# Turning the MLP operand row by row behind the out-projection, preparing the first head earlier, and scalar forms of small products

## Chip, cores and metric

One core of a Trainium2 chip. The metric is the device time of one launch in microseconds (us); a program's time is the median of its runs.

## What is computed

One step of a streaming encoder trunk with two layers, on 1024 prompt rows and 32 sample rows of width 1024, in float32. Cut to what matters here:

```python
def layer_norm(x):
    mu = jnp.mean(x, axis=-1, keepdims=True)
    var = jnp.mean(jnp.square(x - mu), axis=-1, keepdims=True)
    return (x - mu) * lax.rsqrt(var + LN_EPS)
# per layer:  mix  = three groups of attention heads A, B, C (6 + 5 + 5 heads of 64)
#             sub-layer: x <- LayerNorm(alpha * x + gate(c) * sublayer(LN0(x) * (1 + scale(c)) + shift(c)))
# sublayer 1: concat(group_rms(A), group_rms(B), group_rms(C)) @ w_out
# sublayer 2: squared-ReLU MLP, 1024 -> 4096 -> 1024
# group A: p = exp(s - m) / (sum(exp(s - m)) + exp(sink - m)), with a learned sink for each head
```

LN0 is a LayerNorm without gain, so each layer has two norms behind one another: that of the sub-layer's sum (with gain and bias), and that of the next sub-layer's input (with scale and shift). Newest keys and values of all rows are outputs as well.

## The kernel before

All products of matrices run in three passes on the tensor engine: each float32 operand is split into a rounded part and the rest (`hi` and `lo`), and hi x hi, lo x hi and hi x lo are summed in PSUM. The splitting is work of ACT, DVE and POOL (GpSimd). Rows are handled in 9 row tiles: 8 of 128 prompt rows (NPT = 8) and one of 32 sample rows (NTT = 9, index NPT). The activations are also kept turned (columns on the partitions) as `u_hi` and `u_lo`.

Each layer is a series of blocks, and a block ends only when all engines have ended theirs:

- Projections (SP's list at L1014 to L1050, `low_parts` and `products` on POOL, `project` on PE, `query` and the value copies of L1245 on DVE). Queries and keys come out turned, values by row tile. While values are projected, the keys are turned back (L1095), copied by DVE to `k_stage` (L1253, two halves per row tile, `k_st` in the code) and stored by SP (`store_k`); the copy for tile t waits until the stores of tile t-1 have read the stage. In the same time the sums of the conditioning matrices are made: SP loads `w_ada_v` (`sp_conditions`, L283), and each such load waits until DVE's products of an earlier one (L292) are done. SP is one list worked off in order: a wait in it holds all behind.
- Prompt attention. For each of 16 heads POOL splits queries and values (L1402 to L1418), SP loads a bias (`bias`), POOL masks its corners by two memsets, PE scores (L1440), DVE adds the bias and takes the row's maximum (L1564, `logits`), ACT takes exponentials, PE turns the probabilities and multiplies by the values. The first head's keys are split by ACT (L1492) and DVE (L1536) in this block; then DVE makes `minus_sink`, `ident_r` and `causal_r` (L1538 to L1541). PE's first score waits for the two last named. At the end of each head of group A, DVE adds `esk` to `den`, 128x8 at once (L1589).
- Sample attention.
- Out-projection block (L1936 on). The operand is turned column tile by column tile (`turned_feed`), interleaved with the first three row tiles' matmuls; then PE does row tiles 3 to 8 one after another (L1982), each as soon as DVE has read the PSUM of the row tile three before. Per row tile DVE multiplies by the gate, adds to the old rows and takes mean and variance (`sum_rows`: L744, L746, L387, L389, L755); ACT takes the root of the variance (`roots`: L689, L691); DVE refines it (`refine`: L761, L763, L765, L768 or L770); ACT applies the norm (`norm`, L702); POOL applies gain and bias (`chain_pool`: L676, L678); ACT sums the rows and their squares (`second_sums`, L709 to L713, and `second_roots`), DVE refines (`second`), and ACT applies the second norm. The sample's tile comes last and is done by DVE alone. SP loads the old rows, then the first MLP chunk (`w_raw`, 1 MB, chunk UP0), then stores the rows between the norms (L659). POOL splits chunk UP0 when its chain is done.
- MLP block (L2080 on). It starts by turning the operand: `turned_feed` again, PE transposing a column tile of all rows (L436), ACT reading it, DVE splitting it, and PE multiplying with chunk UP0 (L453). Chunk UP0+1 is loaded at the block's start and split by POOL when the operand is done. Then the MLP runs chunk by chunk (L378).
- Between the layers, and at the end, a block of the same chain on the MLP's result (`chain_dve`, `chain_act`, `chain_pool`). Between the layers POOL also splits weights (L357, L359) in between; at the end there is no second norm.

The orders on ACT and DVE in the chain:

```python
for k in range(NTT if final else NPT + 3):          # ACT
    if k < NTT: roots(k)
    if 2 <= k < NPT + 2 and not final:
        second_sums(k - 2); second_roots(k - 2)
    if k < NPT:
        act.wait_ge(f_fig, NTT * u + k + 1); norm(k, f_yn)
    if k >= 3 and not final:
        ...
        norm(k - 3, f_xn)
for k in range(NTT):                                # DVE
    sum_rows(k)
    if k >= 3 and not final: second(k - 3)
    ...
    refine(k, None, f_fig)
```

Of the kernel before, what the change touches and what calls it, by code (L numbers as in the profile page):

```python
# [17 lines left out]
F32 = mybir.dt.float32  # L18
# [48 lines left out]
def build(nc, io):  # L67
# [28 lines left out]
    with ExitStack() as ctx:  # L96
# [62 lines left out]
        u_lo = at("u_lo", U0 + 33792, [P, KT, T], F32R)  # L159
        qk = at("qk_t", Q0, [P, Q_TILES + K_TILES, T])  # L160
# [32 lines left out]
        ks_hi = [at(f"keys_hi{s}", D0 + 4096 * s, [P, SEQ], F32R) for s in range(2)]  # L193
        ks_lo = [at(f"keys_lo{s}", D0 + 8192 + 4096 * s, [P, SEQ], F32R) for s in range(2)]
# [3 lines left out]
        q_st = [at(f"queries{s}", W0 + 4096 * s, [P, SEQ], F32R) for s in range(2)]  # L198
        bias_h = [at(f"bias{s}", W0 + 8192 + 4096 * s, [P, SEQ]) for s in range(2)]
# [347 lines left out]
        f_st = [S(f"rows_stored{i}") for i in range(4)]  # L547
# [17 lines left out]
        GROUPS = ((0, 384), (384, 320), (704, 320))  # L565

# [85 lines left out]
        def chain_stores(sp, u, dst, first, last):  # L652

            for t in range(first, last):
                if t < NPT:
                    sp.wait_ge(f_x1, NPT * u + t + 1)
                else:
                    sp.wait_ge(f_last, u + 1)
                sp.dma_start(dst(t), x_all[0:rows_of(t), t, :]).then_inc(f_st[t % 4], 16)  # L659

        def stored(t, u):

            return 16 * ((3 if t % 4 == 0 else 2) * u + t // 4 + 1)

        def chain_stored(sp, uses):

            for i in range(4):
                sp.wait_ge(f_st[i], 16 * uses * (3 if i == 0 else 2))
# [62 lines left out]
        def chain_dve(own, u, rows, loaded, gate, after_sums, final):  # L731
# [25 lines left out]
            def refine(t, minus_mean, done):  # L757
# [7 lines left out]
                own.did(dve.tensor_tensor(scale, scale, r0, ALU.mult))  # L765
# [3 lines left out]
                else:  # L769
                    ins = dve.tensor_tensor(shift, minus_mean, scale, ALU.mult)  # L770
# [40 lines left out]
            dve.wait_ge(f_st[0], stored(NPT, u))  # L811
# [112 lines left out]
        for l in range(DEPTH):  # L924
# [60 lines left out]

            with nc.Block() as block:
                @block.sync
                def _(sp):
# [64 lines left out]
                def _(pool):  # L1053
# [24 lines left out]
                    for n in range(2, IN_CH):  # L1078
                        low_parts(n)
                        if n < 8:  # L1080
                            products(done, done + (4, 4, 3, 4, 4, 1)[n - 2])
                            done += (4, 4, 3, 4, 4, 1)[n - 2]

# [57 lines left out]
                def _(act):  # L1141
# [46 lines left out]
                    high_part(9)  # L1188

                @block.vector  # L1190
                def _(dve):
# [107 lines left out]
                    query(6)  # L1299
                    query(7)  # L1300
# [14 lines left out]
            span = {"a": 2, "b": 5, "c": NPT}  # L1315
# [12 lines left out]
            with nc.Block() as block:  # L1328
                @block.sync
                def _(sp):  # L1330
                    def bias(hn):
                        g, h = heads[hn][0:2]
                        if hn >= 2:
                            sp.wait_ge(d_lg, NPT * (hn - 1))
                        if g == "a":
                            dst, src = bias_h[hn % 2][:, 0:2 * P], bass.AP(scr_a.tensor, h * P * EXT_A + 127,
                                                                           [[EXT_A - 1, P], [1, 2 * P]])
                        elif g == "b":
                            dst, src = bias_h[hn % 2][:, 0:5 * P], bass.AP(scr_b.tensor, (l * BH + h) * (P * EXT_B) + 127,
                                                                           [[EXT_B - 1, P], [1, 5 * P]])  # L1340
                        else:
                            if h == 0:
                                sp.wait_ge(b_fout, 32)
                            dst, src = bias_h[hn % 2][:].rearrange("p (i t) -> p i t", t=P), \
                                bass.AP(scr_f.tensor, h * P, [[0, P], [CH * P, NPT], [1, P]])
                        sp.dma_start(dst, src).then_inc(d_bias[hn % 2], 16)

# [962 lines left out]
```

## Time and profile before

| what | us |
|---|---|
| median of 3 runs (lowest, highest) | 3181.93 (3179.59, 3183.39) |
| the profiled execution, its own time | 3183.84 |
| span of that execution in the trace | 3182.1 |
| TensorE (PE) busy | 2924.9, 92% of the span |
| DVE, POOL, ACT busy | 1581.2, 1525.1, 875.0 |

In layer 0 the projections end and prompt attention starts at 345.1 us, the out-projection block begins at 642 and the MLP block at 792.3, the block between the layers at 1553; layer 1 follows some 1565 us behind. The last block begins at 3119. The time of a run is about 1.7 us more than the span, which the trace doesn't show. In a timeline row the first number is the start, the second the duration; the brackets say how long the engine was idle before and what released it. A wait of the tensor engine that names "PEq L1936" ended with the end of the block before.

### The profile page before, as it was taken

The page shows a single profiled execution, that of the slowest core. Times are in us where ns is not written, and L with a number is a line of the kernel's source. Part 1 is how long each engine was busy: PE and PEld are TensorE (multiplying, and loading weights), DVE is VectorE, ACT ScalarE, POOL GpSimd, SP SyncE. Part 2 cuts the span into 40 slices and gives each one's busy share as a digit, 9 for nine tenths or more (in the row PEclk, how much of TensorE's full clock was granted, in tenths as well). Part 3 has the DMA queues.
Part 4 walks back from the last instruction along what each step waited for, and adds up shares of the span by engine and source line. Part 5 has one row for each costly group of instructions (what it writes and reads, how often), then busy time and mean ns, then how long its engine had stood idle before and what let it go on. Part 6 is the DMA issues. An engine that isn't in the chain of part 4 may idle for free. (4 is left out here: it accounts for less than half of the span.)

```text
span 3182.1 us, 46999 instructions
## 1 busy us (share of the span) xinstructions
PE 2924.9 (92%) x18646; PEld 2792.0 (88%) x18646; DVE 1581.2 (50%) x3177; ACT 875.0 (27%) x1710; POOL 1525.1 (48%) x716
## 2 busy tenths in 40 slices
PE   5999899887999999999979998998979999999993
PEld 5999789675999999999979897985859999999993
DVE  6552587556433333333775518775653333333347
ACT  1341476425210010011253307663341010001001
POOL 2693497235333443434339818953334443444334
PEclk5999899988999999999769999997989999999996
DMA  5441211431111111110534502114211111111112
GB/s 227 166 167 60 73 48 44 142 114 58 58 41 53 40 52 40 45 47 26 208 142 145 175 14 87 53 45 148 108 55 54 40 53 40 53 40 50 42 47 89
DMA packets 117352, 253.63 MB, mean 80 GB/s; under 512 B 42564, under 2 KB 78952, under 8 KB 103700
## 3 DMA queue, kind: packets, MB, share of 16 engines
q1 hardware_dynamic: 110868, 228.58, 21.0%
q10 hardware_dynamic: 6336, 23.07, 2.1%
q8 instruction: 94, 1.54, 0.2%
q14 instruction: 54, 0.44, 0.0%
HBM read 217.19 MB, written 42.19 MB: 82 GB/s over the span
## 5 line engine op out<-in xcount | busy, mean ns | idle before, releaser
L378 PE MATMUL psum<-u_hi,w_hi 128*128 128x352 f32 x2016 | 650.8, 323 | 3.8 <-DVE v_rows L1245 3.8
L378 PE MATMUL psum<-u_lo,w_hi 128*128 128x352 f32 x2016 | 651.7, 323 | 0.0
L378 PE MATMUL psum<-u_hi,w_lo 128*128 128x352 f32 x2016 | 650.9, 323 | 0.0
L2177 DVE SCALAR_TENSOR_TENSOR acc_t<-psum,mods,acc_t 128x704 f32<-128x704 f32 x720 | 376.2, 578 | 275.0 <-PE psum L378 275.0
L378 PE MATMUL psum<-h_hi,w_lo 128*128 128x352 f32 x1536 | 495.3, 322 | 0.0
L378 PE MATMUL psum<-h_lo,w_hi 128*128 128x352 f32 x1536 | 495.0, 322 | 0.0
L378 PE MATMUL psum<-h_hi,w_hi 128*128 128x352 f32 x1536 | 494.3, 322 | 0.0
L357 POOL CAST w_hi<-w_raw 128x2048 fp32r<-128x2048 f32 x72 | 136.4, 1894 | 638.5 <-DVEq L2170 357.3
L2160 DVE TENSOR_TENSOR h_relu<-h_relu 128x1056 f32<-128x1056 f32 x64 | 112.2, 1754 | 634.2 <-ACT h_relu L2150 634.2
L378 PEld LDWEIGHTS psum<-u_hi,w_hi 128*128 128x128 f32 x2016 | 379.3, 188 | 5.1 <-issue 4.8
L378 PEld LDWEIGHTS psum<-u_lo,w_hi 128*128 128x128 f32 x2016 | 379.6, 188 | 0.0
L378 PEld LDWEIGHTS psum<-u_hi,w_lo 128*128 128x128 f32 x2016 | 379.1, 188 | 0.0
L2150 ACT ACTIVATE h_relu<-psum 128x1056 f32<-128x1056 f32 x64 | 67.4, 1054 | 1102.3 <-PE psum L378 1094.7
L359 POOL TENSOR_TENSOR w_lo<-w_raw,w_hi 128x2048 fp32r<-128x2048 f32 x72 | 359.2, 4989 | 5.8
L1072 POOL TENSOR_TENSOR ada_products<-w_ada_b,c_rows 128x1024 f32<-128x1024 f32 x88 | 239.1, 2750 | 128.7 <-DVE u_lo L499 96.9
L2097 POOL TENSOR_TENSOR h_lo<-h_relu,h_hi 128x1056 fp32r<-128x1056 f32 x64 | 158.2, 2472 | 284.0 <-ACT h_hi L2152 274.4
L378 PEld LDWEIGHTS psum<-h_hi,w_hi 128*128 128x128 f32 x1536 | 289.4, 188 | 0.0
L378 PEld LDWEIGHTS psum<-h_lo,w_hi 128*128 128x128 f32 x1536 | 289.1, 188 | 0.0
L378 PEld LDWEIGHTS psum<-h_hi,w_lo 128*128 128x128 f32 x1536 | 288.5, 188 | 0.0
L1472 PE MATMUL psum<-v_parts,probs_hi 128*128 128x128 f32 x840 | 199.0, 272 | 8.1 <-DVE o_head L1582 5.7
L1472 PE MATMUL psum<-v_parts,probs_lo 128*128 128x128 f32 x840 | 203.6, 278 | 0.0
L1572 DVE TENSOR_TENSOR probs_lo<-psum,probs_hi 128x512 fp32r<-128x512 f32 (+1 forms) x336 | 157.4, 488 | 90.3 <-ACT probs_hi L1519 85.7
(270 smaller groups left out, 5572.0 us busy)
## 6 DMA issues: line engine op xcount, KB each, us to landing
w_raw<-in_w_all SPq DMA_DIRECT2D x86, 1024.0 KB, 4.8
w_ada_b<-in_w_ada_t ACTq DMA_DIRECT2D x44, 512.0 KB, 3.5
w_ada_v<-in_w_ada_t SPq DMA_DIRECT2D x20, 512.0 KB, 3.3
row_tiles<-in_x_prompt SPq DMA_DIRECT2D x16, 512.0 KB, 12.9
scr_o<-o_head SPq DMA_DIRECT2D x32, 256.0 KB, 2.7
row_tiles<-scr_o SPq DMA_DIRECT2D x16, 512.0 KB, 8.9
x_between_norms<-row_tiles SPq DMA_DIRECT2D x16, 512.0 KB, 2.6
mlp_rows<-x_between_norms SPq DMA_DIRECT2D x16, 512.0 KB, 7.2
```

What stands on the lines that cost most here:

```text
L357: pool.tensor_copy(hi[:, 0:c], raw[s][:, 0:c]).then_inc(pool_step, 1)
L359: pool.tensor_tensor(lo[:, 0:c], raw[s][:, 0:c], hi[:, 0:c].bitcast(F32), ALU.subtract).then_inc(pool_step, 1)
L378: mm = pe.matmul(out[:, b, :], w[s][:, c:c + P], a[:, k, b * NB:(b + 1) * NB], start=(k == 0 and w is w_hi and a is a_hi), stop=(k == n - ...
L1072: pool.tensor_tensor(ada_prod[c][:], ada_b[i % 2][:], c_rows[:, c, :], ALU.mult).then_inc(b_prod, 1)
L1472: mm = pe.matmul(psum[:, 6 + n % 2, 0:2 * HD], p[n % 2][:, b, :], v, start=(b == 0 and p is pt_hi), stop=(b == nb - 1 and p is pt_lo))
L1572: own.did(dve.tensor_tensor(pt_lo[n % 2][:, c:c + w, :], psum[:, 4 + g % 2, 0:w * P].rearrange("p (b c) -> p b c", c=P), pt_hi[n % 2][:, c ...
L2097: pool.tensor_tensor(h_lo[par][:, m, :], h_r[m][:], h_hi[par][:, m, :].bitcast(F32), ALU.subtract).then_inc(h_rdy, 1)
L2150: act.activation(h_r[m][:].rearrange("p (b c) -> p b c", c=NB), lin[m], ACT.Relu).then_inc(h_ev[m], 1)
L2160: dve.tensor_tensor(h_r[m][:], h_r[m][:], h_r[m][:], ALU.mult).then_inc(h_sqd, 1)
L2177: ins = dve.scalar_tensor_tensor(a, y, mods[:, 40 + m, c:c + 1], a, ALU.mult, ALU.add)
```

## The change

Four parts.

1. Projections: SP stores the keys of tiles 6, 7 and 8 ahead of the values of tiles 2, 5 and 8, and the tenth load of conditioning weights stands behind the values of tile 2 instead of ahead of the last weight chunk of the values. (Cut: `load_bias` and `mask_bias` are the bodies of SP's `bias` and POOL's memsets, as functions.)

```diff
                     store_k(5)
-                    sp_conditions(sp, "B", l, 9, 10)
                     sp_weights(sp, l, 7, 1)
                     for t in range(NTT):
                         sp.wait_ge(b_ev, V_EV - NTT + t + 1)
-                        store("v", t, v_tok[:, t, :], b_vout)
                         if t % 3 == 2:
                             store_k(6 + t // 3)
+                        store("v", t, v_tok[:, t, :], b_vout)
+                        if t == 2:
+                            sp_conditions(sp, "B", l, 9, 10)
                     sp_weights(sp, l, 8, 2)
+                    sp.wait_ge(b_bias, 16 * (BH + (AH if l == 0 else 0)))
+                    sp.wait_ge(raw_free, IN_CH + 2)
+                    load_bias(sp, l, 0)
```

2. The first head's keys and queries are split, and its bias is loaded and masked, in the projection block; the buffers are moved so that this is possible. PE's wait for `ident_r` and `causal_r` moves to the first head of group C. The sum with `esk` becomes 8 operations with a scalar operand (L1589).

```diff
+                    act.wait_ge(b_ev, K_EV)
+                    act.wait_ge(raw_free, IN_CH + 1)
+                    for a in (a_first, 64 - a_first):
+                        act.activation(ks_hi[0][a:a + 64, :], first_keys, ACT.Copy).then_inc(d_first_hi, 1)
...
                     query(6)
+                    for i, a in enumerate((a_first, 64 - a_first)):
+                        dve.wait_ge(d_first_hi, i + 1)
+                        dve.tensor_tensor(ks_lo[0][a:a + 64, :], first_keys, ks_hi[0][a_first:a_first + 64, :].bitcast(F32),
+                                          ALU.subtract).then_inc(d_first, 1)
+                    dve.wait_ge(raw_free, IN_CH + 2)
+                    dve.wait_ge(b_ev, V_EV + 1)
+                    q, hi = qk[a_first:a_first + 64, heads[0][2], 0:SEQ], q_st[0][a_first:a_first + 64, :]
+                    cond.did(dve.tensor_copy(hi, q))
+                    cond.settle()
+                    dve.tensor_tensor(q_st[0][64 - a_first:128 - a_first, :], q, hi.bitcast(F32), ALU.subtract).then_inc(d_qb, 1)
                     query(7)
...
-                    pe.wait_ge(d_rounded, 2)
                     scores(0)
...
-                                own.did(dve.tensor_tensor(den[:, c], den[:, c], esk[:, c], ALU.add))
...
+                                    own.did(dve.tensor_scalar(den[:, q:q + 1], esk[:, q:q + 1], den[:, q:q + 1], None, ALU.add))
```

3. In `refine`, for all three blocks that use it, two products become operations with a scalar operand; L761 and L768 stay as they are.

```diff
-                own.did(dve.tensor_tensor(scale, scale, r0, ALU.mult))
+                own.did(dve.tensor_scalar(scale, scale, r0, None, ALU.mult))
                 own.settle()
                 if minus_mean is None:
                     ins = dve.scalar_tensor_tensor(shift, mvb[0:r, t, 0:1], -1.0, scale, ALU.mult, ALU.mult)
                 else:
-                    ins = dve.tensor_tensor(shift, minus_mean, scale, ALU.mult)
+                    ins = dve.tensor_scalar(shift, minus_mean, scale, None, ALU.mult)
```

4. The out-projection block gets orders of its own, `out_act` and `out_dve`. Row tiles are worked in the order `ROWS` = 0, 1, sample, 2 to 7. The MLP operand is turned row tile by row tile (`turn_tile`) between the halves of later row tiles; ACT and DVE each read one half of a turned tile twice (`read_half`, rounded and not), and POOL makes the low part (`low`). PE does two thirds of the first MLP chunk (`first_up`, columns of 352 each) in this block and one third at the start of the MLP block, whose own turning goes. POOL splits chunk UP0 first, into other buffers. In the MLP block the load of chunk UP0+2 waits for that last third.

```diff
+                    pool.wait_ge(t_lo, 2 * (KT + 1))
+                    pool.wait_ge(raw_in[0], UP0 * 8 + 16)
+                    pool.tensor_copy(up_hi[:], raw[0][:, 0:CW]).then_inc(pool_step, 1)
+                    pool.wait_ge(pool_step, 2 * UP0 + 1)
+                    pool.tensor_tensor(up_lo[:], raw[0][:, 0:CW], up_hi[:].bitcast(F32), ALU.subtract).then_inc(pool_step, 1)
...
-                    chain_pool(own, USE, 0, NPT)
-                    pool.wait_ge(f_last, USE + 1)
-                    pool_weights(pool, UP0, 1)
+                    chain_pool(own, USE, 0, 4)
+                    low(0)
+                    chain_pool(own, USE, 4, 5)
+                    low(1)
+                    chain_pool(own, USE, 5, 6)
+                    low(2)
+                    low(3)
+                    chain_pool(own, USE, 6, 7)
+                    for t in range(4, NPT):
+                        low(t)
...
+                    def turn_tile(p):
+                        t = ROWS[p]
...
+                        if p == NPT - 1:
+                            pe.wait_ge(f_ev, NTT * USE + NTT)
+                        elif p >= 1:
+                            seen = p if p < NPT else NPT - 1
+                            pe.wait_ge(t_read, FED + sum(q < NPT for q in ROWS[:seen]))
+                            pe.wait_ge(u_half, seen)
+                        if t < NPT:
+                            pe.wait_ge(f_xn, NTT * USE + t + 1)
...
+                    pe.wait_ge(f_gate, 2)
+                    for p in range(3, NTT):
+                        pe.wait_ge(f_ev, NTT * USE + p - 2)
                         for half in range(2):
                             for k in range(KT):
-                                mm = depth(t, k, half)
+                                mm = depth(p, k, half)
+                            if half == 0 and p >= 6:
+                                turn_tile(2 * p - 11)
                         mm.then_inc(f_mm, 1)
+                        if p >= 5:
+                            turn_tile(2 * p - 10)
+                    pe.wait_ge(w_ready, UP0 + 1)
+                    pe.wait_ge(f_ev, NTT * USE + NTT - 1)
+                    pe.wait_ge(t_lo, FED + 3)
+                    first_up(pe, 0)
+                    turn_tile(NPT - 1)
+                    pe.wait_ge(t_lo, FED + 6)
+                    first_up(pe, 1)
+                    turn_tile(NPT)
...
+            def out_act(act, u, junk_rows):
...
+                for t in range(2):
+                    roots(t)
+                    first_norm(t)
+                roots(2)
+                second_sums(0)
+                second_norm_of(0)
+                roots(3)
+                first_norm(2)
+                second_sums(1)
+                second_norm_of(1)
+                roots(NTT)
+                for t in range(3, NPT):
+                    second_sums(t - 1)
+                    roots(t + 1)
+                    first_norm(t)
+                    second_norm_of(t - 1)
+                    for q in {4: (0, 1), 5: (2,), 6: (3, 4), 7: (5,)}.get(t, ()):
+                        read_half(q)
+                second_sums(NPT - 1)
+                second_norm_of(NPT - 1)
+                read_half(NPT - 2)
+                read_half(NPT - 1)
...
+            def out_dve(own, u):
...
+                step(0)
+                step(1)
+                step(2)
+                normed(x, t, None)
+                gained(t, f_last)
+                second(0)
+                step(3)
+                second(1)
+                own.settle()
+                first_figures(t)
...
+                normed(x, t, f_xs)
+                for q in range(4, NTT):
+                    step(q)
+                    second(q - 2)
+                    if q == 5:
+                        read_half(0)
+                        read_half(1)
+                    elif q == 6:
+                        read_sample()
+                        read_half(2)
+                    elif q >= 7:
+                        for t in {7: (3, 4), 8: (5,)}[q]:
+                            read_half(t)
+                dve.wait_ge(f_yn, NPT * u + NPT)
+                gained(NPT - 1, f_x1)
+                read_half(NPT - 2)
+                second(NPT - 1)
+                read_half(NPT - 1)
...
                     sp_weights(sp, l, UP0 + 1, 1)
+                    sp.wait_ge(h_mm, 2)
                     sp_weights(sp, l, UP0 + 2, 2 * MLP_BLK - 2)
```

`second_norm_of(t)` waits for the refined figures of `second(t)`; `second_sums(t)` for POOL's gain and bias of tile t; `first_norm(t)` for `refine`; `step(p)` is `sum_rows` and `refine` of the row tile at place p.

## Rows read from the trace of the kernel before

**Rows 1.** What the tensor engine waits for, whole span: us in total, times, longest

```profile
PE psum L429 <- PEq L1936: 39.8, 2, 19.9
...
PE psum L1440 <- DVE causal_r L1541: 22.7, 2, 11.4
...
PE psum L1095 <- DVE k_stage L1253: 10.7, 2, 5.7
```

**Rows 2.** Timeline of SP, projections of layer 0: start, duration, instruction

```profile
227.37 0.34 SPq L283 DMA_DIRECT2D w_ada_v<-in_w_ada_t  x1
...
230.24 0.53 SPq L1005 DMA_DIRECT2D out_p_b_k<-k_stage  x1
```

**Rows 3.** Timeline of DVE, projections of layer 0 (brackets: idle before)

```profile
219.35 0.55 DVE L1253 COPY k_stage<-psum 128x384 f32<-128x384 f32 x1
...
239.37 0.56 DVE L1253 COPY k_stage<-psum 128x384 f32<-128x384 f32 x1 [11.19 <-DMA out_p_b_k<-k_stage]
...
242.45 3.27 DVE L292 CUSTOM_DVE_ANT_0 ada_products_v<-w_ada_v,c_rows 128x1024 f32<-128x1024 f32 x1
```

**Rows 4.** Timeline of DVE, start of prompt attention, layer 0

```profile
342.34 1.26 DVE L1209 TENSOR_SCALAR qk_t<-psum 128x1056 f32<-128x1056 f32 x1 [10.74 <-PE psum L378]
...
347.48 3.71 DVE L1536 TENSOR_TENSOR keys_lo<-qk_t,keys_hi 64x1024 fp32r<-64x1024 f32 x2 [3.30 <-ACT keys_hi L1492]
...
352.43 1.06 DVE L1541 TENSOR_SCALAR causal_r<-causal 128x128 fp32r<-128x128 f32 x1
354.52 0.48 DVE L1564 CUSTOM_DVE_ANT_0 logits<-psum,bias,minus_sink 128x256 f32<-128x256 f32 x1 [1.04 <-PE psum L1440]
```

**Rows 5.** Timeline of POOL, the same stretch

```profile
350.19 2.04 POOL L1418 TENSOR_TENSOR v_parts<-v_rows,v_parts 128x512 fp32r<-128x512 f32 x1
```

**Rows 6.** DVE instructions by line, prompt attention, layer 0: busy us, mean ns

```profile
L1589 DVE TENSOR_TENSOR denominator<-denominator,exp_sink 128x8 f32<-128x8 f32 x6 | 2.5, 410 | 0.0
```

**Rows 7.** Timeline of DVE, last block, first row tile

```profile
3128.39 0.15 DVE L755 TENSOR_SCALAR row_figures<-tile_mean_var 128x1 f32<-128x1 f32 x1
...
3129.64 2.20 DVE L765 TENSOR_TENSOR row_figures<-row_figures 128x1 f32<-128x1 f32 x1
```

**Rows 8.** Timeline of POOL, last block, first row tile

```profile
3127.06 2.35 POOL L676 TENSOR_TENSOR row_tiles<-row_tiles,ln_gain 128x1024 f32<-128x1024 f32 x1 [46.50 <-ACT row_tiles L702]
3129.49 2.34 POOL L678 TENSOR_TENSOR row_tiles<-row_tiles,ln_bias 128x1024 f32<-128x1024 f32 x1
```

**Rows 9.** Timeline of DVE, block between the layers

```profile
1586.97 4.24 DVE L765 TENSOR_TENSOR row_figures<-row_figures 128x1 f32<-128x1 f32 x1
```

**Rows 10.** Busy time by engine in the out-projection's last six row tiles (us, instructions)

```profile
705.30:772.50 67.20, 67.15 (x290) 50.22 (x288) 44.25 (x99) 37.80 (x72) 35.60 (x15) 1.00 0.27 105
```

**Rows 11.** Timeline of POOL, out-projection block, layer 0

```profile
709.07 2.40 POOL L676 TENSOR_TENSOR row_tiles<-row_tiles,ln_gain 128x1024 f32<-128x1024 f32 x1 [38.83 <-ACT row_tiles L702]
...
783.90 4.50 POOL L359 TENSOR_TENSOR w_lo<-w_raw,w_hi 128x2048 fp32r<-128x2048 f32 x1
```

**Rows 12.** Timeline of ACT, out-projection block, layer 0

```profile
719.27 1.06 ACT L709 ACTIVATE row_products<-row_tiles 128x1024 f32<-128x1024 f32 x1
...
722.40 1.23 ACT L702 ACTIVATE row_tiles<-row_tiles,row_figures 128x1024 f32<-128x1024 f32 x1
```

**Rows 13.** DMA issues of 701.6 to 717: KB each, us from issue to landing

```profile
w_raw<-in_w_all SPq DMA_DIRECT2D x1, 1024.0 KB, 14.8
```

**Rows 14.** Timeline of PE, start of the MLP block, layer 0

```profile
817.82 1.04 PE L436 MATMUL psum<-ident,row_tiles 128*128 128x128 f32 x8
...
835.20 0.33 PE L453 MATMUL psum<-u_lo,w_hi 128*128 128x352 f32 x1
835.36 0.36 PE L378 MATMUL psum<-u_hi,w_hi 128*128 128x352 f32 x1
```

**Rows 15.** Timeline of DVE, out-projection block, layer 0

```profile
750.24 1.23 DVE L744 TENSOR_TENSOR psum<-psum,gate_prompt 128x1024 f32<-128x1024 f32 x1 [5.30 <-PE psum L1982]
...
754.58 0.22 DVE L761 SCALAR_TENSOR_TENSOR row_figures<-row_figures 128x1 f32<-128x1 f32 x1
```

More of the change, by code:

```diff
@@ L192, in build @@
         D0 = W0 + 2 * WB
-        ks_hi = [at(f"keys_hi{s}", D0 + 4096 * s, [P, SEQ], F32R) for s in range(2)]
-        ks_lo = [at(f"keys_lo{s}", D0 + 8192 + 4096 * s, [P, SEQ], F32R) for s in range(2)]
+        ks_hi = [at(f"keys_hi{s}", (W0, D0)[s], [P, SEQ], F32R) for s in range(2)]
+        ks_lo = [at(f"keys_lo{s}", (W0, D0)[s] + 4096, [P, SEQ], F32R) for s in range(2)]
         pt_hi = [at(f"probs_hi{s}", D0 + 16384 + 4096 * s, [P, 8, P], F32R) for s in range(2)]
@@ L197, in build @@
         lg = [at(f"logits{s}", A0 + 4096 * s, [P, D]) for s in range(3)]
-        q_st = [at(f"queries{s}", W0 + 4096 * s, [P, SEQ], F32R) for s in range(2)]
-        bias_h = [at(f"bias{s}", W0 + 8192 + 4096 * s, [P, SEQ]) for s in range(2)]
+        q_st = [at(f"queries{s}", (W0 + WB, D0 + 8192)[s], [P, SEQ], F32R) for s in range(2)]
+        bias_h = [at(f"bias{s}", (W0 + WB, D0 + 8192)[s] + 4096, [P, SEQ]) for s in range(2)]
         o_h = [at(f"o_head{s}", U0 + 49152 + 2048 * s, [P, NPT, HD]) for s in range(2)]
@@ L546, in build @@
         f_fig2, f_last = S("f_second_figures"), S("f_sample_x1")
-        f_st = [S(f"rows_stored{i}") for i in range(4)]
+        u_half, f_xs = S("u_half_read_vector"), S("f_sample_normed")
+        f_st = [S(f"rows_stored{i}") for i in range(4)] + [S("sample_rows_stored")]
         act_step, pool_row = S("act_steps"), S("pool_rows")
@@ L810, in chain_dve @@
             refine(t, None, None)
-            dve.wait_ge(f_st[0], stored(NPT, u))
+            dve.wait_ge(f_st[4], stored(NPT, u))
             normed(t, f_xn)
@@ L1488, in _ @@
                     load_tables(act)
-                    first = heads[0]
-                    a0 = 64 * first[3]
-                    for a in (a0, 64 - a0):
-                        act.activation(ks_hi[0][a:a + 64, :], qk[a0:a0 + 64, Q_TILES + first[4], 0:SEQ], ACT.Copy)\
-                            .then_inc(d_first_hi, 1)
                     act.activation(q_smp[:], qk[:, 0:Q_TILES, SEQ:T], ACT.Copy)
@@ L1925, in build, with bank_pair, turned_halves, first_up @@
             USE = min(l, 1)
-            def bank_pair(t):
-                return wide[t % 3]
+            FED = 2 * (KT + 1)
+            ROWS = (0, 1, NPT) + tuple(range(2, NPT))
+            def bank_pair(p):
+                return wide[p % 3]
+            def turned_halves(p):
+                return (2, 5) if p == NPT - 1 else (6, 7)
+            def first_up(pe, b):
+                for m in range(2):
+                    for k in range(KT):
+                        c = 256 * k + P * m
+                        for w, a in ((up_hi, u_hi), (up_lo, u_hi), (up_hi, u_lo)):
+                            mm = pe.matmul(lin[m][:, b, :], w[:, c:c + P], a[:, k, b * NB:(b + 1) * NB],
+                                           start=(k == 0 and w is up_hi and a is u_hi), stop=(k == KT - 1 and a is u_lo))
+                    if b == 2:
+                        mm.then_inc(h_mm, 1)
```

251 lines of the change are left out of this document (196 added, 55 removed).

## Prediction

> **What bounds the kernel now.** I began with the list of what TensorE (PE) waits for, because PE is busy nearly all the span and only its gaps can be won. [rows 1] show three that this change touches: 19.9 us per layer ahead of the MLP (L429, waiting for the block before to end), 11.4 us per layer ahead of prompt attention (L1440, waiting for `causal_r` on DVE), and 5.7 us in one layer's projections (L1095, waiting for `k_stage`). The matmuls of the MLP itself run without gaps and are not touched. Then I read each gap's neighbourhood on the queue or engine that ends it.
>
> **Projections: the keys are stored ahead of the values.** DVE could have staged keys of tile 6 when the copy of 219.35 had ended, but the copies of the next tiles wait for `k_stage` to be read out, and the one at 239.37 waited 11.19 us for that store [rows 3]. SP stood at a wait for tile 8's condition products, issued the next load of that kind at 227.37, then a weight load and value stores, and the key store only at 230.24 [rows 2]. After the change no condition load stands ahead of tile 6's keys: their store can go out at about 220, 10 us earlier, so the copy that waited is free before its data are. What is late next are DVE's own condition products of tile 9. Their load now follows tile 2's value stores; its issue cannot precede the end of tile 8's products at 227.3 either, so it goes out then and lands about 3 us later; before, the second of its two products took 3.27 and ended at 245.7 [rows 3], and PE was past this place some 1.8 us behind that, at 247.5. Starting at 230.6, two products of at most 3.3 end by 237.2, and PE is past at about 239. I take 9 us in layer 0 and 8 in layer 1, whose gap here is 5.0 (10.7 less 5.7 [rows 1]): **-17**. Bounds: the gap alone, 5.7 + 5.0 = -10.7; all 10 us of the store's delay twice, -20. The chunk-7 load is issued earlier too, and its split on POOL stays ahead of PE by some 6 us.
>
> **First head's parts ahead.** The attention block of layer 0 starts at 345.1. DVE's `keys_lo` takes 3.71 us from 347.48, then three constants follow, the last from 352.43 for 1.06; only then may PE score, and the first softmax step (L1564) runs at 354.52 [rows 4]. After the change the keys and queries of head 0 are split in the projection block: two ACT copies, and on DVE those 3.71 us, a copy and one more subtraction, some 6 us, between two query tiles; DVE idles 10.74 us before its last query tile [rows 4], and POOL and SP idle too. They cost nothing there; without that cover, 6 us per layer. The first bias load and its two memsets also lie in that idle time. PE now scores at the block's start, 8.4 us earlier, but DVE's softmax step still stands behind the constants, and POOL now begins with the value parts, whose second half ran 2.04 us [rows 5]; next to that a DVE constant took 1.06. First softmax step: start + 3.3 (three constants, one of them behind that half) = 348.4 instead of 354.5, so 6.1 us. Against it, the sink sum of 6 instructions x 0.410 us [rows 6] becomes 48 narrow ones per layer; these overlap, so that each takes between half and all of the 0.15 of a 128x1 form [rows 7]: 3.6 to 7.2 against 2.5, of which I take the lower end: +1.1. Net -5 per layer, **-10**; bounds -4 (PE gains only what DVE's constants allow if all three are held) and -18 (the whole 8.4 plus a little).
>
> **Scalar forms of small products.** In the last block L765, a 128x1 product of two SBUF columns, takes 2.20 us and ends at 3131.84, exactly with POOL's L678 (3129.49 + 2.34); L755, a tensor-scalar form, took 0.15 in the middle of POOL's L676 (3127.06 + 2.35); both in [rows 7, 8]. So the new form is not held; but L768 right behind it, again with two SBUF columns, keeps its form and is held until 3131.84 instead. The gain is one operation's 0.15 to 0.2 us in 8 tiles: **-1.5**. The two ends: 0, and -15 if L768 also went free (8 x 1.9). Between the layers it differs: POOL splits weights there and L765 lay 4.24 us behind such a split [rows 9], twice. With L765 and L770 of the preceding pair free, DVE comes to L768 about 2.3 us earlier, before the split's second half starts, and only one short hold is left. POOL's chain (2 x 2.36 per tile and two splits of 6.4) then sets the pace; following it through the eight tiles gives **-5.5**, ends 0 and -9.6.
>
> [...]
>
> **The MLP operand, turned behind the out-projection.** This is the large part. Before: PE runs the out-projection's last six row tiles without a gap, 67.2 us or 11.2 per tile [rows 10]; then 19.9 us of nothing [rows 1]; then the turned feed and the first chunk, until the second chunk begins at 835.36 [rows 14]. After, turning a tile (8 transposes, 1.04) and the first two thirds of the chunk (48 matmuls x 0.16 = 7.7 each) [rows 14] move ahead of the block's end; if nothing waited, the second chunk would begin at 772.5 + 9 x 1.04 + 3 x 7.7 + a last tile's chain, about 810 to 819.
>
> But the chain of a row tile gets slower, at three places. First, POOL now splits chunk UP0 ahead of the chain. Its load is issued at 701.75, behind all rows, and lands 14.8 us later, at 716.5 [rows 13]; cast and subtraction (4.50 the latter, [rows 11]) make 6.4: the chain starts at 723 instead of 709.07 [rows 11]. Second, ACT's order. Before, the sums of tile k-2 stand ahead of the first norm of tile k, so two tiles are in flight. After, the sums of tile t-1 stand ahead of the norm of tile t, and need POOL's result of t-1: per tile POOL 4.9, sums 3.1 (719.27 to 722.40), norm 1.23 [rows 12], roots and refine 1.2, together about 10.5 one behind the other, and DVE's step of 4.3 (750.24 to 754.58) [rows 15] in between where it is late. Third, ACT and DVE read tile 0's halves only behind the second norm of tile 3. Followed through: POOL's tiles 0 and 1 until 733, tile 2 from 738, tile 3 from 754 to 757, its sums until 763 to 765, its second norm at about 768, the reads at 770. PE meets this at `turn_tile(1)`, which stands between the halves of the seventh row tile and needs both reads: PE arrives at 746.6 and goes on at 770, **24 us** of gap, more than the 19.9 removed. From there POOL's low parts stand between its chain passes as well, and each further row tile comes only every 16 us (row half, step 4.3, roots, refine, norm, reads 1.45, turn 1.04, row half 5.6): the last row tile ends at 810, first third of the chunk 819, second third 823 to 832 (it waits for low(5)), last turn 833, reads and low(7) 839. That is the block's end, against 792.3 before. Then the last third (7.7 to 10), while the load of chunk UP0+1, issued only now, takes 5.1 and its split 6.4: the second chunk begins at 847 to 851 instead of 835.4. The load of UP0+2 now waits for that third; the 23 us of the second chunk cover it. I take +13 per layer, **+26**: the middle of the hand-followed times, less the 2 us by which the same following overstates the block before. The unknown in it is the price of one 128x128 read, 8 of which make a half on each engine. A 128x1 form at 0.15 [rows 7] bounds it below, a 128x1024 norm at 1.23 [rows 12] above; I take 0.18, near the lower end, as it has an eighth of the elements. 0.3 would add 4 per layer.
>
> **The sum.** -17 - 10 - 1.5 - 5.5 + 26 = -8. Against the profiled run of 3183.84 us that is 3176; it stood 1.9 above the median of the runs, so **3174**. A measurement can tell about 0.2% (6.4 us) from no change.
>
> **Rivals.** (a) The block flows as laid out: ACT and DVE reach tile 0's reads before PE comes to `turn_tile(1)`. For it: DVE idled 5.30 us before the row tile of 750.24 [rows 15]. Against it: the order of waits above is fixed in code. The second chunk would begin at 806 to 819, -16 to -29 per layer: 3182 - 34 - 45 = about 3103. Chance 0.12. (b) Slower: the reads. they stand inside the 16 us loop; at 0.4 us each, between my bounds, a half costs 3.2 instead of 1.45, five times in PE's way, +9 per layer beyond the +13: -34 + 44 = +10, 3192. It decides if PE's gap at `turn_tile(1)` passes 26 us and the second chunk starts after 853; from +17 per layer on the gains are eaten up. Chance 0.22. (c) L768 isn't held after all, or the order of POOL and DVE falls better: -15 and -4 more, 3155. Chance 0.10. (d) The scalar forms and the early parts gain nothing (held, or hidden): -17 - 4 + 26 = +5, 3187. Chance 0.10. The forecast has 0.46, its own range 3162 to 3184.
>
> The range reaches from (c) with part of its bounds, 3148, to 3196 past (b); it leaves (a) and tails out, about 0.2. Faster by over 0.2%: (a), (c) and two thirds of the forecast, 0.53. Slower: most of (b) and a part of (d), 0.23. The rest, 0.24.
>
> **What would show it.** In the changed profile: a PE gap of some 24 us inside the out-projection, ended by an ACT or DVE read; POOL's first chain pass at about 723; the first split of the MLP block ending after the block's first third; L1440's first matmul within 1 us of the block's start, but softmax 3 us later; no PE wait for `k_stage`; in the last block a short L765 and an L768 of about 2 us. A gap below 8 us at `turn_tile(1)` would prove the largest term wrong, and the time would lie below 3150; an L768 of 0.16 beside a busy POOL the other.

## The result, and the profile after

The changed kernel is slower: 3194.84 us median (3188.18 to 3196.80, 8 runs) against 3180.98 (3176.74 to 3183.39, 8 runs), a ratio of 1.0042 with a 95% interval of 1.0033 to 1.0051. The profiled execution took 3195.36 us, its span is 3193.5. Line numbers in the rows of a run are those of its own kernel, so those of the changed kernel differ from those of before.

Stage by stage, from the ends and starts of PE's work in the two timelines (both layers together; the third row reaches from PE's last matmul of prompt attention to the MLP's last one, since nothing in the MLP itself changed):

| stage | before | after | difference | forecast |
|---|---|---|---|---|
| projections | 542.2 | 521.7 | -20.5 | -17 |
| prompt attention | 466.7 | 456.5 | -10.2 | -10 |
| sample attention, out-projection, MLP | 1950.8 | 1997.9 | +47.1 | +26 |
| between the layers | 86.0 | 82.2 | -3.9 | -5.5 |
| last block | 66.0 | 64.5 | -1.5 | -1.5 |

The sum, with +0.4 ahead of the first projection, is +11.4, which is the difference of the spans. Four of five terms came out within 4 us; one decided.

What PE waits for in the out-projection block and the start of the MLP block of layer 0 (total us, times, longest), in answer to [rows 1]:

```profile
PE psum L2314 <- ACT u_hi L2025: 30.3, 2, 26.3
PE psum L1968 <- PEq L2191: 5.7, 1, 5.7
PE psum L1968 <- POOL u_lo L2233: 4.6, 1, 4.6
PE psum L2314 <- issue: 2.2, 2, 1.5
PE psum L381 <- POOLq L364: 1.2, 1, 1.2
```

The 19.9 us at the block's end are gone, and 26.3 stand inside the block, at the turning of the second tile (L2314), waiting for ACT's reads (L2025). The waits for `k_stage` and `causal_r` are gone too. Prompt attention starts 3.1 us behind PE's last projection, with the end of the block:

```profile
PE psum L1476 <- PEq L1018: 6.2, 2, 3.1
```

POOL in that block, in answer to [rows 11] (start, duration):

```profile
701.89 4.62 POOL L2224 TENSOR_TENSOR w_up_lo<-w_raw,w_up_hi 128x2048 fp32r<-128x2048 f32 x1
706.83 2.41 POOL L705 TENSOR_TENSOR row_tiles<-row_tiles,ln_gain 128x1024 f32<-128x1024 f32 x1 [0.33 <-POOL w_up_lo L2224]
...
726.94 2.41 POOL L705 TENSOR_TENSOR row_tiles<-row_tiles,ln_gain 128x1024 f32<-128x1024 f32 x1 [9.07 <-ACT row_tiles L1991]
...
743.32 2.36 POOL L705 TENSOR_TENSOR row_tiles<-row_tiles,ln_gain 128x1024 f32<-128x1024 f32 x1 [11.49 <-ACT row_tiles L1991]
...
757.82 2.35 POOL L2233 TENSOR_TENSOR u_lo<-u_rows_turned,u_hi 128x1024 fp32r<-128x1024 f32 x1 [9.72 <-ACT u_hi L2025]
```

All stages are 16.5 us earlier here than before (PE ends sample attention at 624.06 instead of 640.60), so 706.83 is the forecast's 723. The passes of tiles 2 and 3 start 15 and 16 us behind the passes ahead of them, with POOL idle for 9 and 11 us ahead of each: one tile in flight, as the order on ACT has it.

A part of the first of these gaps was made on DVE, which does the sample's norm, gain and bias in this stretch, beside POOL's split and first passes:

```profile
709.29 2.97 DVE L2106 TENSOR_SCALAR row_tiles<-row_tiles,row_figures 32x1024 f32<-32x1024 f32 x1
712.37 3.25 DVE L2113 TENSOR_TENSOR row_tiles<-row_tiles,ln_gain 32x1024 f32<-32x1024 f32 x1
715.64 3.31 DVE L2115 TENSOR_TENSOR row_tiles<-row_tiles,ln_bias 32x1024 f32<-32x1024 f32 x1
```

```profile
720.12 1.24 ACT L1991 ACTIVATE row_tiles<-row_tiles,row_figures 128x1024 f32<-128x1024 f32 x1 [5.14 <-DVE row_figures L2092]
```

In the kernel before, where the sample's tile came last, the same three took 0.80, 1.21 and 1.21 us. Ahead of them two of the sample's refining operations were held, L2083 for 3.81 us and L2090 for 2.29. ACT had its sums of tile 0 and waited 5.1 us for DVE's refining of that tile, which stands behind the sample in DVE's list.

ACT, PE and DVE where PE's gap of 26 us ends:

```profile
753.74 1.22 ACT L1991 ACTIVATE row_tiles<-row_tiles,row_figures 128x1024 f32<-128x1024 f32 x1
754.87 1.48 ACT L2025 ACTIVATE u_rows_turned<-psum,mods 128x128 f32<-128x128 f32 x4
756.23 1.50 ACT L2025 ACTIVATE u_hi<-psum,mods 128x128 fp32r<-128x128 f32 x4
```

```profile
757.79 1.97 PE L2314 MATMUL psum<-ident,row_tiles 128*128 128x128 f32 x8 [26.28 <-ACT u_hi L2025]
```

```profile
753.47 1.36 DVE L2135 TENSOR_SCALAR u_rows_turned<-psum,mods 128x128 f32<-128x128 f32 x4
754.75 1.36 DVE L2135 TENSOR_SCALAR u_hi<-psum,mods 128x128 fp32r<-128x128 f32 x4
```

Here is a number that failed: eight reads of 128x128 take 2.86 us on ACT (754.87 to 757.73) and 2.64 on DVE, that is 0.36 and 0.33 each, where 0.18 was taken. They stand behind the second norm of tile 3 (L1991), as the prediction had it.

The last block, first row tile on DVE and POOL, in answer to [rows 7, 8]:

```profile
3141.98 0.38 DVE L790 SCALAR_TENSOR_TENSOR row_figures<-row_figures 128x1 f32<-128x1 f32 x1 [0.50 <-ACT row_figures L720]
3142.39 0.15 DVE L792 TENSOR_SCALAR row_figures<-row_figures 128x1 f32<-128x1 f32 x1
3142.58 0.21 DVE L794 TENSOR_SCALAR row_figures<-row_figures 128x1 f32<-128x1 f32 x1
3142.83 1.95 DVE L797 SCALAR_TENSOR_TENSOR row_figures<-tile_mean_var,row_figures 128x1 f32<-128x1 f32 x1
```

```profile
3142.42 2.34 POOL L707 TENSOR_TENSOR row_tiles<-row_tiles,ln_bias 128x1024 f32<-128x1024 f32 x1
```

L794, once L765 with 2.20 us, now takes 0.21 beside POOL's operation; L797, the next operation, takes 1.95 and ends with it. The hold moved by one instruction.

### The profile page after: what moved, and what is told of

Read it like the earlier page. It is cut to its first block and busy times, and to the rows that moved or that the text cites. A ratio compares the mean times of both kernels' runs of the same rounds, so it can differ in the third digit from the quotient of the medians.

```text
span 3193.5 us, 47368 instructions
## 1 busy us (share of the span) xinstructions
PE 2919.7 (91%) x18646; PEld 2785.4 (87%) x18646; DVE 1616.3 (51%) x3365; ACT 902.1 (28%) x1822; POOL 1551.3 (49%) x724
## 5 line engine op out<-in xcount | busy, mean ns | idle before, releaser
L362 POOL TENSOR_TENSOR w_lo<-w_raw,w_hi 128x2048 fp32r<-128x2048 f32 x70 | 350.3, 5004 | 5.6
```

The lines of the kernel that those rows point to most:

```text
L362: pool.tensor_tensor(lo[:, 0:c], raw[s][:, 0:c], hi[:, 0:c].bitcast(F32), ALU.subtract).then_inc(pool_step, 1)
```

## The experiments

The stage that went wrong is compared below by one number for each kernel: the time from PE's last prompt attention matmul to the MLP's last, both layers, as in the table's third row (before 1950.8, changed kernel 1997.9). A difference of 4 us in it says nothing: the kernel with the new order of SP's list alone (below), whose code is the same there as before, took 1946.8.

**Which part costs.** All parts but the turning: the blocks of the out-projection and the MLP are those of before, the rest is the changed kernel.

> All parts of the change but the turning behind the out-projection: the out-projection block and the start of the MLP block are those of before. Theory (each part stands by itself; the turning alone loses, about 24 us per layer by the traces): the projections keep about -20, prompt attention -10, the block between the layers -4, the last block -1.5, so about 3145 us, 36 below before and 50 below the changed kernel, and the MLP block begins 19.9 us behind PE's last out-projection matmul as before. Rival (the parts pay for each other: buffers that were moved for the early first head, or the new store order, cost time in the out-projection block): 3160 or more, with a longer out-projection block than before.

Measured: 3147.83 us (3143.93 to 3148.62), ratio to before 0.9893 (0.9876 to 0.9909). The stage takes 1951.4 us, as before; PE's gap ahead of the MLP is back at 20.2. The other parts do not need the turning: together they gained 33 us, and the turning lost 47.

**Where the projections' gain comes from.** The kernel before with SP's order alone:

```diff
-                    sp_conditions(sp, "B", l, 9, 10)
                     sp_weights(sp, l, 7, 1)
...
-                        store("v", t, v_tok[:, t, :], b_vout)
                         if t % 3 == 2:
                             store_k(6 + t // 3)
+                        store("v", t, v_tok[:, t, :], b_vout)
+                        if t == 2:
+                            sp_conditions(sp, "B", l, 9, 10)
```

> The kernel before with the order of SP's list in the projections alone: keys of tiles 6 to 8 ahead of values, the tenth conditioning load behind the values of tile 2. Theory (the whole gain of the projections is this order): the gap at k_stage goes, the projections are 11 us shorter in layer 0 and 9 in layer 1, 3180.9 - 20, about 3161, and prompt attention still starts with a gap of 11.4 us. Rival (a part of the gain comes from the first head's work in the projection block, or from the bias load): less than 12 us in all.

Measured: 3159.29 us (one run), 20.7 below before. The projections are 11.2 and 8.5 us shorter, and attention starts as it did before:

```profile
342.58 0.58 PE L1441 MATMUL psum<-keys_hi,queries 128*128 128x256 f32 x1 [11.36 <-DVE causal_r L1542]
```

So the order of SP's list is the whole gain of the projections (the stores and the moved load were not tried apart), and the first head's work there costs nothing: with it, in the kernel without the turning, they are just as short.

**The split ahead of the chain.** POOL's list with the split of chunk UP0 moved (its lines written here as `split_up`):

```diff
-                    split_up()
-                    chain_pool(own, USE, 0, 4)
+                    chain_pool(own, USE, 0, 4)
+                    split_up()
                     low(0)
```

> The changed kernel, but POOL splits the first MLP chunk behind the gain and bias passes of tiles 0 to 3 instead of ahead of them. Theory (the order on ACT and DVE sets the pace, the late POOL start is only a part): PE's gap at the second turned tile shrinks from 26 to about 20 us and the second MLP chunk begins 5 to 6 us earlier per layer, about -11 us, 3184. Rival (the split ahead of the chain is what breaks it): the gap goes below 8 us and 20 us or more per layer come back, 3155 or less.

Measured: 3185.70 us (one run); the gap at the second turned tile (L2312 here) is 19.7 us, the stage 1986.6, 11 less. The split's place is a part of the loss, and a small one; the rival falls. POOL starts its passes earlier in this run, and the sample's norm, gain and bias on DVE are back at 0.80, 1.21 and 1.21 us; which of the two gave more is not shown.

**The first read.** ACT's and DVE's `read_half(0)` moved ahead of the loops:

```diff
                 roots(NTT)
+                read_half(0)
...
                 normed(x, t, f_xs)
+                read_half(0)
```

(The same reads go from their old places.)

> The changed kernel, but ACT and DVE read the first turned tile earlier: ACT right behind the roots of the sample's second norm, DVE right behind the sample's second norm. Nothing else moves. Theory (the 26 us gap at the second turned tile only shows where PE meets a chain of norms that is late anyway): the gap shrinks to about 6 us, another of about 18 us comes at the third turned tile, and the second MLP chunk begins only 6 to 7 us earlier per layer: -13 us, about 3182. Rival (this one wait is the loss): the gap shrinks by 20 us and the time by as much per layer, -40 us, about 3155.

Measured: 3188.56 us (one run), the stage 1989.0, 9 less. The two gaps in PE's timeline:

```profile
737.14 1.09 PE L2315 MATMUL psum<-ident,row_tiles 128*128 128x128 f32 x4 [8.09 <-DVE u_hi L2136]
...
758.42 0.84 PE L2315 MATMUL psum<-ident,row_tiles 32*128 32x32 f32 x6 [12.47 <-ACT u_hi L2025]
```

The 26 us fell to 8, and 12.5 came at the next turned tile: 18 us off the longest gap gave some 4 per layer. The expectation was right in kind and 2 to 3 us per layer too high. Here a gap of PE is where the delay shows, not where it is made.

**The price of the reads.** Each half read twice over, on ACT and on DVE:

```diff
-                    for dst in (u_raw, u_hi):
+                    for dst in (u_raw, u_hi, None, u_raw, u_hi):
```

(`None` is a wait for the reads before it.)

> The changed kernel, but ACT and DVE read every turned half twice over (the second time with the same result), so a half costs 5.9 us instead of 2.9 on ACT and 5.5 instead of 2.7 on DVE. Theory (the reads lie in the loop that paces PE, about five of them one behind the other): the second MLP chunk begins 13 to 16 us later per layer, +28 us, 3223. Rival (the reads lie beside other work, and what was lost is lost in waits for norms): +6 us or less in all.

Measured: 3223.62 us (one run), 28.8 above the changed kernel; the stage takes 2028.6, 30.7 more. The reads lie in the loop some five times one behind the other in each layer: 2.9 us more per half on ACT made some 15 per layer.

**The order.** The same work, in another order on three engines. The lists, with r = `roots`, F = `first_norm`, s = `second_sums`, N = `second_norm_of`, h = `read_half`; P = `step`, S = `second`, G and Y = the sample's first and second norm, R = `read_sample`, Z = the last gain and bias; c = a chain pass, U = the split, l = `low`:

```
ACT  r0 r1 F0 r2 s0 F1 r3 r9 s1 F2 N0 r4 N1 h0 F3 s2 r5 F4 h1 s3 r6 N2 N3 s4 F5 h2 N4 s5 r7 h3 F6 h4 N5 s6 r8 h5 N6 F7 h6 s7 N7 h7
DVE  P0 P1 P2 G P3 Y S0 S1 P4 h0 P5 S2 h1 P6 S3 R S4 h2 P7 h3 h4 S5 P8 S6 h5 Z S7 h6 h7
POOL c0 c1 c2 U c3 c4 l0 l1 c5 l2 l3 c6 l4 l5 l6 l7
```

> The changed kernel with the same work, but another order on ACT, DVE and POOL in the out-projection block: a turned half is read as soon as it is there, the first norms run ahead of the sums of earlier tiles so that two tiles are in flight, and POOL splits the chunk behind the passes of tiles 0 to 2. PE's order is as it was. Theory (the order is what costs): PE's gap at the second turned tile falls below 10 us, the second MLP chunk begins about 30 us earlier per layer, -55 to -65 us, about 3135. Rival (the work itself is too long: reads, low parts and holds between DVE and POOL fill the engines): -15 us or less, 3180 or more.

Measured: 3135.87 us (3133.57 to 3138.88), ratio to before 0.9859 (0.9843 to 0.9876), 59.0 below the changed kernel; the stage takes 1940.1. PE's waits of layer 0's block and MLP start:

```profile
PE psum L2285 <- ACT u_hi L2025: 6.9, 3, 2.8
PE psum L1968 <- PEq L2164: 5.7, 1, 5.7
PE psum L1968 <- POOL u_lo L2197: 1.8, 1, 1.8
PE psum L381 <- POOLq L364: 1.2, 1, 1.2
```

With the same instructions the longest wait for a read is 2.8 us. ACT reads tile 0 (h0) ahead of the first norm of tile 3 instead of behind the second norm of that tile, and F3, F4 run ahead of s2, s3, so that POOL has the next tile while ACT sums. The sample's norm, gain and bias no longer fall beside POOL and take 0.80, 1.21 and 1.21 us again. The order is the cause, by what waits for what and by what it puts side by side.

**The hold in the refining.** The two operations left with two SBUF inputs, in scalar form too, in both places where the refining is written:

```diff
-own.did(dve.scalar_tensor_tensor(scale, r0, v, r0, ALU.mult, ALU.mult))
+own.did(dve.tensor_scalar(scale, v, r0, r0, ALU.mult, ALU.mult))
...
-ins = dve.scalar_tensor_tensor(shift, mvb[0:r, t, 0:1], -1.0, scale, ALU.mult, ALU.mult)
+ins = dve.tensor_scalar(shift, mvb[0:r, t, 0:1], scale, -1.0, ALU.mult, ALU.mult)
```

> The changed kernel, with the first and last operation of the refining (L790 and L797 of the changed kernel, each with two SBUF columns as inputs) also written as tensor_scalar with scalar operands. Theory (an operation with two SBUF inputs is held until POOL's operation ends, a tensor_scalar on columns is not): in the last block none of the refining takes more than 0.3 us, a row tile goes from 6.3 to about 4.5 to 4.9 us and the block ends 11 to 15 us earlier; between the layers 0 to 4 less, in the out-projection blocks 1 to 2 less each, so 3194.8 - 13 to 22, about 3178. Rival (the refining is held whatever its form while POOL works, since L792 and L794 only happened to come at free moments): the hold moves to another operation of the refining and the time stays within 3 us.

Measured: 3172.24 us (one run), 22.6 below the changed kernel: 10.4 in the last block (54.1 us), 7.7 between the layers (74.5), 8.5 in the stage of the out-projection, while the projections, whose code is the same, took 3.8 more. The 8.5 are more than expected: in the changed kernel the sample's L2083 and L2090 alone had been held 3.8 and 2.3 us there. The refining and POOL's operation beside it, in the last block:

```profile
3129.36 0.27 DVE L790 TENSOR_SCALAR row_figures<-row_figures 128x1 f32<-128x1 f32 x1 [0.51 <-ACT row_figures L720]
3129.67 0.15 DVE L792 TENSOR_SCALAR row_figures<-row_figures 128x1 f32<-128x1 f32 x1
3129.85 0.21 DVE L794 TENSOR_SCALAR row_figures<-row_figures 128x1 f32<-128x1 f32 x1
3130.10 0.21 DVE L797 TENSOR_SCALAR row_figures<-tile_mean_var,row_figures 128x1 f32<-128x1 f32 x1
3130.23 1.21 DVE L775 SCALAR_TENSOR_TENSOR row_tiles<-mlp_rows,psum 128x1024 f32<-128x1024 f32 x1
```

```profile
3129.82 2.36 POOL L707 TENSOR_TENSOR row_tiles<-row_tiles,ln_bias 128x1024 f32<-128x1024 f32 x1
```

A tile now takes 4.35 us on DVE (3125.89 to 3130.23 between two L775) instead of 6.1. The rest of what was expected is lost at the end, where the sample's wide operations run beside POOL's last passes:

```profile
3160.69 2.76 DVE L814 TENSOR_SCALAR row_tiles<-row_tiles,row_figures 32x1024 f32<-32x1024 f32 x1
3163.55 3.17 DVE L830 TENSOR_TENSOR row_tiles<-row_tiles,ln_gain 32x1024 f32<-32x1024 f32 x1
3166.76 1.21 DVE L832 TENSOR_TENSOR row_tiles<-row_tiles,ln_bias 32x1024 f32<-32x1024 f32 x1
```

L814 took 0.80 in the changed kernel, L830 1.21.

**Together.** The reordered kernel with the refining in scalar form and a cheaper read on ACT, with an order made for these times:

```diff
+                    for k in range(KT // 2):
+                        ins = act.activation(u_raw[:, k, c], psum[:, turned_halves(p)[0], k * P:(k + 1) * P], ACT.Identity,
+                                             bias=mods[:, 24 + k, 0:1], scale=mods[:, 32 + k, 0:1])
+                    own.did(ins)
+                    own.settle()
+                    act.activation(u_hi[:, 0:KT // 2, c], u_raw[:, 0:KT // 2, c], ACT.Copy).then_inc(t_read, 1)
```

```
ACT  r0 F0 r1 r2 F1 s0 r3 N0 r9 F2 s1 r4 s2 F3 N1 h0 r5 F4 h1 N2 s3 r6 F5 s4 h2 N3 N4 s5 h3 r7 F6 h4 N5 h5 r8 s6 F7 N6 s7 N7 h6 h7
DVE  P0 P1 P2 P3 G S0 Y P4 S1 h0 P5 S2 h1 P6 R h2 S3 S4 h3 P7 S5 h4 P8 h5 S6 Z h6 S7 h7
POOL c0 c1 c2 U c3 l0 c4 l1 c5 l2 c6 l3 l4 l5 l6 l7
```

> The reordered kernel with three more things: all of the refining in scalar form, ACT reading a turned half once from PSUM and rounding it from SBUF in one operation (about 2.1 us instead of 2.9), and an order that fits these times. Theory: the second MLP chunk begins another 8 to 10 us earlier per layer than in the reordered kernel, the last block is 11 to 15 us shorter and the block between the layers 0 to 4: 3135.9 - 16 to 20 - 13 - 2, about 3103. Rival (POOL's passes become the bound once DVE isn't held): no more than -15 us, 3120 or more.

Measured: 3095.61 us (3093.55 to 3099.82), ratio to before 0.9738 (0.9724 to 0.9751). The stage takes 1921.6 us, 29 less than before. PE's waits of layer 0's block and MLP start:

```profile
PE psum L1968 <- PEq L2165: 5.6, 1, 5.6
PE psum L381 <- POOLq L364: 3.0, 1, 3.0
PE psum L2286 <- ACT row_tiles L1991: 2.8, 3, 1.1
PE psum L2232 <- ACT gate_sample L2323: 1.1, 1, 1.1
```

What is left are the block's end, with the last tile's reads and low part, and POOL's split of chunk UP0+1. The rival falls. What each of the three things brings of the 18.5 us that the stage gains over the reordered kernel was not measured.

The counterpart without turning, the kernel of the first experiment with the same scalar refining:

> The kernel without the turning, with all of the refining in scalar form; beside the reordered kernel of 3095.6 us it shows what turning behind the out-projection is worth in a good order. Theory (turning well ordered saves 15 to 17 us per layer; scalar refining saves 10 in the last block and 8 between the layers here too, and at most 2 per layer in the out-projection, whose tail has two held operations): 3147.8 - 18 to 22, about 3128, 30 to 34 us above the reordered kernel. Rival (the scalar forms alone do it, and turning is worth nothing in any order): 3105 or less.

Measured: 3123.70 us (3120.27 to 3126.85), ratio to before 0.9820 (0.9804 to 0.9837). The stage takes 1948.4 us there and 1921.6 with the turning well ordered: turning is worth 13 us per layer, where as written it costs 24. The rival falls.

## Why the prediction was wrong

The sign was wrong, and the time was outside the forecast's own range, though inside the stated one. By its steps:

- **Projections, -17: measured -20.5.** Right in mechanism and place. In the changed kernel the key store went out at 220.11 and the two products of tile 9 ran from 230.86 to 235.87; forecast were 220, 230.6 and 237.2. The gain lies just past the bound of 20.
- **First head's parts, -10: measured -10.2.** PE scores at 334.09, the first softmax step runs at 335.86, 1.8 behind it: DVE's constants were done 2.0 us behind the block's start instead of the 3.3 I allowed, and the sink sum's 48 operations took 6.3 us per layer, not 3.6. Two errors of opposite sign, so the nearness is partly luck. (The DVE constant of 1.06 us that was read as lying beside POOL's value parts started behind them, at 352.43, when L1418 had ended at 352.23.)
- **Scalar forms, -1.5 and -5.5: measured -1.5 and -3.9.** In the last block the hold moved to the next operation, as said. Between the layers it moved too: I had followed it to one short hold, but L790 and L797 together took 30.8 us there, where the same two lines took 9.0 before. All-scalar refining gave the rest.
- **The turning, +26: measured +47.** This is the step that failed, first in one term of its sum: "The unknown in it is the price of one 128x128 read ... I take 0.18, near the lower end". It measured 0.36 on ACT and 0.33 on DVE. The mechanism held: the first chain pass at 723 (measured 706.8, which is 723.4 on before's clock), one tile in flight, PE stopped at the second turned tile. The times are on before's clock, 16.5 us behind the changed kernel's own:

| point | forecast | measured |
|---|---|---|
| POOL's first pass of tile 2 | 738 | 743.5 |
| POOL's first pass of tile 3 | 754 to 757 | 759.9 |
| PE goes on at the second turned tile | 770 | 774.3 |
| first third of the chunk starts | 811 | 817.7 |
| second third starts | 823 | 831.1 |
| last third starts | 839 | 848.2 |
| second chunk starts | 847 to 851 | 859.7 |

Each layer lost 23.5 us where 13 were forecast. The doubled reads give the size of the read's part: 2.9 us more per half made some 15 more per layer, so the 1.45 that the forecast was short makes 7 to 8 of the 10.5 that are missing (an estimate: no run made the reads cheaper in this order).

A part of the rest cannot be the reads. POOL was 5 us behind the forecast at tile 2, before any half was read. There the forecast names no time for the sample's operations on DVE beside POOL, which took 15.6 us (L2083 to L2115 above) where the same five take 3.6 when nothing holds them. And its own working gives less than it took: the middle of 847 to 851 lies 13.6 behind 835.4, and less 2 that is 11.6, not 13. How the remaining 3 us per layer divide is open.

- **Rivals.** Rival (b), the reads at 0.4, with 3192 and a chance of 0.22, is nearest to what happened, by its place, its price (0.36) and both its conditions: a gap above 26 us (26.3, so barely) and a second chunk behind 853 (859.7). Its cost was put among the rivals though a row of this very shape stood in the trace of the kernel before, an ACT copy of 128x128 from PSUM:

```profile
L1519 ACT ACTIVATE probs_hi<-psum 128x128 fp32r<-128x128 f32 x82 | 22.4, 274 | 4.9 <-PE psum L1456 4.0
```

That is 0.27 us without a column's scale and bias; even a form of 128x1 takes ACT 0.20 there (L689, L691), so 0.18 lay below both. Rival (a), that the block flows, failed as written. The reordered kernel comes near it: its longest wait for a read is 2.8 us, but its second chunk starts at 828.7 on before's clock, against (a)'s 806 to 819. The order was most of what kept (a) from being true, not all. Rivals (c) and (d) did not come: L797, once L768, was held (1.95 us), and the early parts and scalar forms gained.
- **Which forms were held.** L797, with two SBUF columns as inputs, took 1.95 us beside POOL's L707 and ended with it (3144.78 against 3144.76). No tensor_scalar of 128x1 took over 0.28 us in any run (the longest, 0.28, is L790 of the kernel with all-scalar refining), so none was held as L797 was.

## What to carry to other kernels

Where four engines hand a tile on to each other, write down each engine's list and follow the tiles through it: with the prices read from the changed kernel's trace, that gave every reordering's time here within 8 us, while PE's longest gap misled (18 us less of it gave 4). Before work is moved behind a running stage, price its smallest repeated operation from a row of the same shape and engine, since a wrong 0.18 us, 8 times per half, made 7 to 8 us per layer (an estimate from the doubled reads). Also ask what a new order puts side by side: the sample's norm, gain and bias took 0.80, 1.21 and 1.21 us at the end of the block and 2.97, 3.25 and 3.31 in the middle of it, beside POOL. And when a wait is taken from one operation in a chain, look at the next one of the same form: here L765's 2.20 us became L797's 1.95, until that was changed too (0.21).

## What was not expected of the hardware

- A read of 128x128 from PSUM costs ACT 0.36 us one behind the other, while an eighth of the 1.24 us of a 128x1024 norm would be 0.15. The copies of L1519 in the kernel before, from PSUM too, take 274, 381, 490 and 598 ns for 128, 256, 384 and 512 columns: 0.11 us for each 128 columns on top of some 0.17 that does not depend on the size (an estimate from these four). Reading once and rounding 128x512 from SBUF in one operation (0.63 us) brought a half from 2.9 to 2.15 us.
- A column product with a column as scalar operand takes 0.21 us (L794), 0.05 more than the form with two tensors when that is not held (0.16, L765 of the kernel before). Writing the two held ones so still won 22.6 us (one run) where POOL works.
- A tensor_scalar is not free of POOL in every shape: of 128x1 none took over 0.28 us in any run, while those of 32x1024 took 2.76 us (L814, kernel with all-scalar refining) and 2.97 us (L2106, changed kernel) beside POOL's passes and 0.80 without.
